# A hybrid decoder layer: half-width weight splits, a convolution tap on another engine, and moved value steps

## The reference, cut to what matters

```python
h  = rms_norm(x) * (1 + scale) + shift
z  = h @ w_in          # att q,k,v,gate | mLSTM q,k | v | o | gate | i,f | merge gates
# branch A: block-sparse softmax attention, 8 heads x 64
# branch B: 4 mLSTM heads, qk dim 128, v dim 256
qk = silu(causal_conv4(qk_pre, w_conv) + b_conv);  k = k * 128 ** -0.5
s  = (q @ k.T) * w;    num = s @ v;    den = s.sum(-1)
h  = num / maximum(abs(den), exp(-m));  h = rms_norm(h) * g * sigmoid(o)
C  = sum_s ws[s] * v[s] k[s]^T
u  = sigmoid(ga) * (ya @ w_att) + sigmoid(gm) * (ym @ w_mlstm);  y = x + gate * (u @ w_out)
```

## Time and profile before

| | us |
|---|---|
| runs shown | 815.5, 823.34, 824.85 |
| median | 823.34 |
| profiled execution | 820.3 |
| its span | 818.6 |
| TensorE busy in it | 728.3 |
| VectorE busy in it | 556.7 |

### The profile page before, as it was taken

How to read it: one execution, slowest core, us unless ns; L and a number is a source line. 1 busy time by engine, 2 the same in 40 slices (tenths; PEclk the granted TensorE clock), 3 DMA queues, 4 the chain that set the end, 5 groups by cost and what they waited for, 6 DMA issues and landing times.

```text
span 818.6 us, 14649 instructions
## 1 busy us (share of the span) xinstructions
PE 728.3 (89%) x5040; PEld 625.2 (76%) x5040; DVE 556.7 (68%) x501; ACT 311.6 (38%) x586; POOL 471.1 (58%) x204
## 2 busy tenths in 40 slices
PE   5889999798987969877999899997899999899993
PEld 1225888577765868776999889887789998899992
DVE  0150359989998897599699699879857458522342
ACT  1422463554526224324244343443232223323454
POOL 3035239446563852765966868678265646667552
PEclk9999799899896989989999999999799999999997
DMA  8974625688876891067557657569327535732202
GB/s 320 331 258 143 193 78 148 193 254 255 269 217 205 259 309 54 1 182 223 165 168 236 172 172 230 157 204 266 90 54 205 167 112 158 240 113 87 78 0 104
DMA packets 156902, 144.69 MB, mean 177 GB/s; under 512 B 7547, under 2 KB 115152, under 8 KB 156852
## 3 DMA queue, kind: packets, MB, share of 16 engines
q1 hardware_dynamic: 142696, 136.10, 55.5%
q10 hardware_dynamic: 14164, 8.07, 3.4%
HBM read 135.10 MB, written 9.11 MB: 176 GB/s over the span
## 4 chain that ended last, share of the span: by engine, by line
PE 34%; DVE 30%; issue 14%; SPq 7%; POOL 6%; DMA 4%; ACT 2%; DVEq 1%; POOLq 0%; ACTq 0%
PE ps L522 21%; DVE sb_arenaA L1600 5%; DVE sb_arenaA L1751 5%; DVE sb_arenaA L1756 4%; PE ps L540 4%; SPq L385 3%; DVE sb_arenaB L1756 3%; POOL sb_wL L1314 3%; SPq L386 3%; DMA sb_arenaA<-in_w_ada 2%; DVE sb_arenaB L1809 2%; DVE sb_arenaA L1604 2%; DVE sb_arenaB L1675 2%; SPq L369 1%; POOL sb_uL L1478 1%
## 5 line engine op out<-in xcount | busy, mean ns | idle before, releaser
L1314 POOL TENSOR_TENSOR sb_wL<-sb_wraw,sb_wH 128x1024 fp32r<-128x1024 f32 (+1 forms) x88 | 223.3, 2539 | 231.1 <-ACT sb_wH L929 222.6
L522 PE MATMUL ps<-sb_hH,sb_wH 128*128 128x260 f32 x1152 | 241.9, 292 | 4.3 <-POOL sb_wL L1314 2.5
L522 PE MATMUL ps<-sb_hL,sb_wH 128*128 128x260 f32 x1152 | 234.9, 286 | 0.0
L522 PE MATMUL ps<-sb_hH,sb_wL 128*128 128x260 f32 x1152 | 234.6, 286 | 0.0
L522 PEld LDWEIGHTS ps<-sb_hH,sb_wH 128*128 128x128 f32 x1152 | 182.0, 193 | 15.7 <-issue 11.9
L522 PEld LDWEIGHTS ps<-sb_hL,sb_wH 128*128 128x128 f32 x1152 | 181.3, 192 | 0.0
L522 PEld LDWEIGHTS ps<-sb_hH,sb_wL 128*128 128x128 f32 x1152 | 180.5, 192 | 0.0
L929 ACT ACTIVATE sb_wH<-sb_wraw 128x1024 fp32r<-128x1024 f32 (+1 forms) x88 | 90.3, 1026 | 228.9 <-PE ps L522 189.7
L1383 POOL TENSOR_TENSOR sb_arenaA<-sb_arenaA 128x2048 f32<-128x2048 f32 x32 | 117.7, 3682 | 10.1 <-DMA sb_arenaA<-in_cache_v 8.2
L1354 POOL TENSOR_TENSOR sb_arenaA<-sb_arenaA 128x2048 f32<-128x2048 f32 x12 | 61.5, 5122 | 35.8 <-DMA sb_arenaA<-in_cache_k 35.8
L1604 DVE TENSOR_REDUCE sb_arenaA<-sb_arenaA 128x2048 f32 (+1 forms) x32 | 72.5, 2280 | 6.8 <-POOL sb_arenaA L1354 4.6
(11 more groups left out here) (343 smaller groups left out, 1058.3 us busy)
## 6 DMA issues: line engine op xcount, KB each, us to landing
sb_wraw<-in_w_in SPq DMA_DIRECT2D x64, 512.0 KB, 4.8
sb_arenaA<-in_cache_k SPq DMA_DIRECT2D x128, 256.0 KB, 3.1
sb_arenaA<-in_cache_v SPq DMA_DIRECT2D x128, 256.0 KB, 3.2
sb_arenaA<-in_w_ada SPq DMA_DIRECT2D x6, 2048.0 KB, 8.8
sb_arenaB<-in_state_C SPq DMA_DIRECT2D x8, 512.0 KB, 3.8
sb_wraw<-in_w_mlstm SPq DMA_DIRECT2D x8, 512.0 KB, 4.1
sb_wraw<-in_w_out SPq DMA_DIRECT2D x8, 512.0 KB, 3.7
sb_arenaB<-in_x_prompt SPq DMA_DIRECT2D x1, 2048.0 KB, 18.2
```

The lines of the kernel that those rows point to most:

```text
L522: last = mm(ps[:, 2 * s + a, 0:HALF], w[:, s, k, :], x[:, k, a * HALF:(a + 1) * HALF], start=(k == 0 and w is wH and x is xH), stop=(k == ...
L1314: tt(wL[:, j % 2, 0:ks], wraw[:, j % 4, 0:ks], wH[:, j % 2, 0:ks].bitcast(F32), ALU.subtract)\
```

## The change

1. The copy of the keys (ScalarE, L1063) and the store of k stand ahead of the scaling of the values.
2. TensorE does tile 4 of the first mLSTM head ahead of the score sums (L828), and tile 5 ahead of L833.
3. `high` and `low` work in two halves of a tile each. The first half of a high part waits only for the first half of the tile two before (`z_half`), and TensorE waits for the second low half in the middle of its tile.
4. The first tap of each convolution, with the bias, is done by ScalarE (`first_tap`), and VectorE waits for it.
5. KSCALE is folded into L1782 and L1790; the two scalings of the keys and their semaphore are gone.
6. On VectorE the value pairs move within a head. In the loop: 6 (of the head before), weights and scores, copy, 0, weighted keys, 2, denominators, scaled output, 4, gate products, gated output. In the first head: 0, 2 and 4 all behind the scaled output.
7. On POOL each value step of the loop moves ahead of one low part: step 6, low 2, step 7, low 3, step 0, low 0, mask, step 1, low 1, step 2, low 2, step 3, low 3, step 4, low 0, step 5, low 1. In the first head step 4 moves ahead of the low part of tile T_ML+9 (tile 1 of the second head), and at the end step 6 ahead of a low part.

SP's order isn't changed. The core of the diff:

```diff
@@ -510,10 +511,13 @@
             tr = nc.tensor.transpose
 
             def ztile(j, n, xH, xL, ks=KT, part_ready=None):
-                pe.wait_ge(lo_done, n + 5)
+                pe.wait_ge(lo_done, 2 * n + 9)
                 pe.wait_ge(z_free, n + 1)
                 s = j % 2
                 for k in range(ks):
+                    if k == ks // 2:
+                        last.then_inc(z_half, 1)
+                        pe.wait_ge(lo_done, 2 * n + 10)
                     if part_ready:
                         pe.wait_ge(part_ready, 2 + k + 1)
                     for w, xs_ in ((wH, (xH, xL)), (wL, (xH,))):
...
@@ -732,7 +737,6 @@
                     ztile(3, n + 3, hH, hL)
                     pe.wait_ge(hn_ev, 4 * h + 1)
                 pe.wait_ge(sg_rdy, 2 * h + 2)
-                pe.wait_ge(qk_rdy, h + 1)
                 pe.wait_ge(ym_done, h + 1)
...
@@ -821,17 +825,17 @@
                     last = tr(ps[0:B, 5 + a, t * P:(t + 1) * P], qkvS[:, 1 + a, t, :], ident[:, :])
             last.then_inc(sel_pe, 1)
             ztile(3, T_ML + 3, hH, hL)
+            ztile(4, T_ML + 4, hH, hL)
 
             pe.wait_ge(ya_done, 1 + PAIRS)
             pe.wait_ge(sel_dve, 2)
             for b in range(B):
                 last = mm(ps[0:B, 7, 0:P], colsel[:, b, :], score[:, b * P:(b + 1) * P], start=(b == 0), stop=(b == B - 1))
             last.then_inc(sel_pe, 1)
-            ztile(4, T_ML + 4, hH, hL)
+            ztile(5, T_ML + 5, hH, hL)
 
             pe.wait_ge(sel_dve, 3)
             mm(ps[:, 7, :], ones[0:B, :], pend.rearrange("p b n -> p (b n)"), start=True, stop=True).then_inc(sel_pe, 1)
-            ztile(5, T_ML + 5, hH, hL)
             pe.wait_ge(sel_act, 1)
             mlstm(0, True)
             with pe.Fori(0, MH - 1) as h:
...
@@ -922,11 +926,13 @@
             chain = Chain(act, act_chain)
             f = nc.scalar.activation
 
-            def high(j, n, quad, ks=KT):
+            def high(j, n, quad, ks=KT, after_short=False):
 
                 act.wait_ge(ld_w[j % 4], 16 * (quad + 1))
-                act.wait_ge(z_done, n + 1)
-                f(wH[:, j % 2, 0:ks], wraw[:, j % 4, 0:ks], ACT.Copy).then_inc(hi_done, 1)
+                for half, used in ((0, z_done if after_short else z_half), (1, z_done)):
+                    part = slice(half * ks // 2, (half + 1) * ks // 2)
+                    act.wait_ge(used, n + 1)
+                    f(wH[:, j % 2, part], wraw[:, j % 4, part], ACT.Copy).then_inc(hi_done, 1)
 
             def leave(j, n, *dests):
                 act.wait_ge(z_done, n + 3)
...
@@ -1057,12 +1063,12 @@
                 high(3, n + 3, quad)
                 weights(0, t)
                 leave(0, n + 2, (vT, ACT.Copy))
-                normalise(0, t)
                 act.wait_ge(kn_mm, t + 1)
                 act.wait_ge(st_k, 16 * t + 16)
                 f(kN, ps[:, 7, :].rearrange("p (j n) -> p j n", j=TT), ACT.Copy).then_inc(kn_ev, 1)
                 act.wait_ge(kn_ev, t + 1)
                 act.dma_start(rows_out(O["k_p"], t), kN).then_inc(st_k, 16)
+                normalise(0, t)
                 high(0, n + 4, quad + 1)
                 if not before:
                     gate_exps()
...
@@ -1076,6 +1082,15 @@
                 leave(1, n + 3, (yaT[:, bass.ds(t, 1), :].rearrange("p o n -> p (o n)"), ACT.Silu))
                 high(1, n + 5, quad + 1)
                 weights(1, t)
+
+            def tap(j, e, h):
+                return vcol[:, bass.ds(h + (V_WC + KT * j + MH * e), 1)]
+
+            def first_tap(e, h):
+
+                act.wait_ge(z_free, T_ML + 8 * h + 3 + e)
+                f(cacc[:, e, :], pre[:, e, 0:T], ACT.Identity, scale=tap(0, e, h),
+                  bias=vcol[:, bass.ds(h + (V_BC + MH * e), 1)]).then_inc(tap_rdy, 1)
 
             attention(0, False)
             with act.Fori(0, PAIRS - 1) as t:
...
@@ -1102,6 +1117,9 @@
             act.wait_ge(ya_done, 1 + PAIRS)
             act.wait_ge(st_k, 16 * (1 + PAIRS))
             act.wait_ge(st_v, 16 * (1 + PAIRS))
+            act.wait_ge(v_one, 2)
+            for e in range(2):
+                first_tap(e, 0)
             for e in range(2):
                 act.wait_ge(cv_rdy, e + 1)
                 f(qkc[:, e, :], cacc[:, e, :], ACT.Silu).then_inc(sg_rdy, 1)
...
@@ -1138,7 +1156,9 @@
                     high(2, n + 2, quad)
                     leave(0, n, (pre[:, 0, 3:3 + NT], ACT.Copy))
                     high(3, n + 3, quad)
+                    first_tap(0, h)
                     leave(1, n + 1, (pre[:, 1, 3:3 + NT], ACT.Copy))
+                    first_tap(1, h)
                     decays(h, False)
                     for e in range(2):
                         act.wait_ge(cv_rdy, 2 * h + e + 1)
...
@@ -1310,11 +1330,13 @@
 
             def low(j, n, ks=KT):
 
-                pool.wait_ge(hi_done, n + 1)
-                tt(wL[:, j % 2, 0:ks], wraw[:, j % 4, 0:ks], wH[:, j % 2, 0:ks].bitcast(F32), ALU.subtract)\
-                    .then_inc(lo_done, 1)
-
-            pool.sem_inc(lo_done, 4)
+                for half in range(2):
+                    part = slice(half * ks // 2, (half + 1) * ks // 2)
+                    pool.wait_ge(hi_done, 2 * n + half + 1)
+                    tt(wL[:, j % 2, part], wraw[:, j % 4, part], wH[:, j % 2, part].bitcast(F32), ALU.subtract)\
+                        .then_inc(lo_done, 1)
+
+            pool.sem_inc(lo_done, 8)
             for slot in range(KV_SLOTS):
                 pool.sem_inc(page_free[slot], 1)
             pool.sem_inc(u_lo, 2)
...
@@ -1401,32 +1423,32 @@
             pool.wait_ge(sel_dve, 8)
             for s in range(4):
                 value_step(s, 0)
+            value_step(4, 0)
             low(1, T_ML + 9)
-            value_step(4, 0)
             value_step(5, 0)
             with pool.Fori(0, MH - 1) as i:
                 h = i + 1
                 n = T_ML + 8 * h
+                value_step(6, h - 1)
                 low(2, n + 2)
-                value_step(6, h - 1)
+                value_step(7, h - 1)
                 low(3, n + 3)
-                value_step(7, h - 1)
+                value_step(0, h)
                 pool.wait_ge(w_exp, h + 1)
                 low(0, n + 4)
                 causal_weights(h)
-                value_step(0, h)
+                value_step(1, h)
                 low(1, n + 5)
-                value_step(1, h)
+                value_step(2, h)
                 low(2, n + 6)
-                value_step(2, h)
+                value_step(3, h)
                 low(3, n + 7)
-                value_step(3, h)
+                value_step(4, h)
                 low(0, n + 8)
-                value_step(4, h)
+                value_step(5, h)
                 low(1, n + 9)
-                value_step(5, h)
+            value_step(6, MH - 1)
             low(2, T_GATE + 2)
-            value_step(6, MH - 1)
             value_step(7, MH - 1)
             for j in range(1, 4):
                 low((j + 2) % 4, T_GATE + j + 2)
...
@@ -1669,8 +1691,7 @@
                 def tap(j):
                     return vcol[:, bass.ds(h + (V_WC + KT * j + MH * e), 1)]
 
-                chain(v.tensor_scalar(acc, pre[:, e, 0:T], tap(0), vcol[:, bass.ds(h + (V_BC + MH * e), 1)],
-                                      ALU.mult, ALU.add))
+                dve.wait_ge(tap_rdy, 2 * h + e + 1)
                 for j in range(1, 4):
                     last = v.scalar_tensor_tensor(acc, pre[:, e, j:j + T], tap(j), acc, ALU.mult, ALU.add)
                     if j < 3:
...
@@ -1772,24 +1791,26 @@
                 if first:
                     choice_sums()
                 else:
-                    dve.wait_ge(sg_rdy, 2 * h + 2)
-                    v.tensor_scalar(qkc[:, 1, :], qkc[:, 1, :], KSCALE, None, ALU.mult).then_inc(qk_rdy, 1)
-
                     value_pair(6, h - 1, False)
                 dve.wait_ge(st_mm, h + 1)
                 dve.wait_ge(w_rdy, h + 1)
                 for k, b, c in ((0, 4, 0), (1, 5, 0), (3, 5, 384), (2, 6, 0)):
-                    last = tt(wt[:, k, 0:T - k * P], wt[:, k, 0:T - k * P], ps[:, b, c:c + T - k * P], ALU.mult)
+                    last = v.scalar_tensor_tensor(wt[:, k, 0:T - k * P], wt[:, k, 0:T - k * P], KSCALE,
+                                                  ps[:, b, c:c + T - k * P], ALU.mult, ALU.mult)
                 last.then_inc(mpt_rdy, 1)
                 dve.wait_ge(z_free, n + 6)
                 v.tensor_copy(vS[:, bass.ds(2 * h, 2), :], mvT[:, :, T:NT])
                 if first:
                     choice_normalise()
+                if not first:
+                    value_pair(0, h, first)
                 dve.wait_ge(kt_mm, h + 1)
                 dve.wait_ge(wsc_rdy, h + 1)
-                tt(kw, ps[:, 6, :].rearrange("p (j n) -> p j n", j=TT), over(wsc[:, :], P), ALU.mult)\
+                v.scalar_tensor_tensor(kw, ps[:, 6, :].rearrange("p (j n) -> p j n", j=TT), KSCALE, over(wsc[:, :], P),
```

(11 more changed lines are left out.)

17 lines of the change are left out of this document (9 added, 8 removed).

## The result

The changed kernel takes 827.15 us (median of 7, 825.93 to 829.96), the kernel before 822.24 (median of 7, 815.5 to 825.32). The change is slower by about 1%, where 839 (815 to 848) was forecast. The profiled execution has a span of 825.4 us, against 818.6 before.

What follows compares the result with a forecast made beforehand. TensorE was busiest (728.3 of 818.6 us), but VectorE set the mLSTM head's 65.6 us period. Terms: 820.3 + 11 (first head) + 6.8 (two heads) + 2.5 (gate stage) − 2 (attention) = 838.6, forecast 839, range 815 to 848.

Steps and rivals of the forecast that it cites:

- attention: Attention stage: key copy ahead of the scaling takes most of L696's 14.1 us wait, little returns; −2 us, bounds −5 and +3.
- tile ahead of the score sums: Ahead of the first mLSTM head: a tile of matmuls fills L828's 6.4 us wait; 4 us gained, bounds 0 and 6.4.
- first head, scores to scores: First mLSTM head: late page release and step 4 make head 1's scores later, +11 us net, bounds +4.7 to +12.2.
- two loop heads: Steady mLSTM heads: VectorE idles twice for POOL's steps and products are blocked; +3.4 us each, bounds −3.1 and +5.
- here the POOL edit bites: First mLSTM head: low half of tile T_ML+9 now stands behind late step 4; TensorE stands 12.5 us before tile 1.
- Into the gate stage: After the last mLSTM head: L1813 comes later, and L846's wait and the sample chain follow; +2.5 us, bounds 0 and +3.
- the case: Whole kernel: the prediction's main outcome, slower, chance 0.60, alone said to reach from 826 to 847 us.
- The signs: mLSTM heads: TensorE idles about 12 us, step 4 about 6 later, two VectorE idles per head, L738 distances 68 to 70.
- Rival A: mLSTM heads: POOL delivers steps in time, waits go, TensorE sets the period at 62.5; 810 us, chance 0.12.
- Rival B: mLSTM heads: even; first head pays only 4.7 us, each steady head is 1 shorter; 821 us, chance 0.22.
- Rival C: All stages: TensorE waits mid-tile for a low half, 0.6 us in every second of 64 tiles; 839 us, chance 0.06.

Runs made afterwards that it cites:

- repeated old orders: Second run of the changed kernel with VectorE's value sums and POOL's value steps in the order of before, in all heads; 801.67 us.

## Why the prediction was right or wrong

By its own terms, profile against profile:

| term | predicted | measured | from |
|---|---|---|---|
| attention | −2 | −9.9 | L816 284.69, now L820 274.83 |
| tile ahead of the score sums | −4 | −3.3 | to L742 of head 0: 30.5, now 27.2 |
| first head, scores to scores | +15 | +13.7 | 71.6, now 85.3 |
| two loop heads | +6.8 | +4.5 | 65.6, now 67.85 each |
| from L742 of head 3 to the end | +2.5 | +1.7 | 300.7, now 302.4 |
| sum | +18.3 | +6.7 | span +6.8 |

*The first head* (+11 with the tile's 4 in it, so +15) was right in mechanism and size. The denominators caught in POOL's row of steps, step 4 at 32.7 us behind the first step (measured 32.0), TensorE's wait of 12.5 (11.4): all stand in the rows above. The emphasis on "here the POOL edit bites" was wrong: with the low part put back ahead of step 4 the scores came only 1.7 us earlier. The step that decides is the release of the pages by pair 0, that is, the denominators ahead of it on VectorE.

*The loop heads* were right nearly row by row: the two idle times (6 and 6.3 forecast, 5.78 and 6.01 measured) with their causes, pages for step 3 and ScalarE's root ahead of the high part. Only the gate products were taken too long, with two full blocks and a half: one full block came (3.80, L1833) and two partial ones, and the head took 67.85 and not 69. The rule of the Trainium skill in "SBUF — State Buffer", "Who interferes with whom", held in the rows shown here, most sharply on the smallest products (3.54 us for 128x4 values). L1816 has only one input and was held up as well (1.79 us for 0.17), which the rule as the prediction put it doesn't cover.

*Into the gate stage* +2.5 was a guess, and its mechanism didn't show: the wait that was to grow shrank (L846's 5.50 us, now L850's 3.9). The next one, L855's of 2.9 us, now L859's, grew to 6.5, and the granted clock from 570 to 705 us was 0.92 and not 0.95. Split at the first L895 (now L899; 123.2 and 120.5 us from the end), the stretch is 4.4 us longer ahead of it and 2.7 shorter behind it, where 0 was forecast. How much of this is the clock stays open.

*Attention* is the term that was mis-sized, by 7.9 of the 11.6 us between the two sums. Its premise, "in that stage VectorE is the busier engine", isn't so. The stage before and after, and TensorE's wait for the scaled weights of the softmax, before and after:

```profile
76.00:285.00 209.00, 188.27 (x1213) 155.56 (x1211) 171.49 (x169) 95.08 (x197) 110.33 (x29) 0.91 0.70 209
```

```profile
76.00:275.00 199.00, 185.69 (x1225) 155.54 (x1223) 158.64 (x169) 96.73 (x215) 104.29 (x47) 0.93 0.74 219
```

```profile
PE ps L626 <- ACT sb_arenaB L1025: 2.1, 3, 0.9
```

```profile
PE ps L631 <- ACT sb_arenaB L1031: 9.9, 4, 3.5
```

TensorE is busy 188.27 of 209 us, VectorE 171.49. Of the 10 us, 7.4 are idle time of TensorE (20.7, now 13.3) and 2.6 are busy time, for about as many matmul records at a granted clock of 0.93 and not 0.91. The waits say what the key copy does: 11.7 us go from L696, and 7.8 come back at L631, since the scaling (L1031) now stands behind the copy. The 3.9 us left over are inside the forecast's −5 and +3. The rest, clock and halves, wasn't in the term. The halves were costed at nothing, on POOL's own time (two of 1.28 against 2.40), and what they do to VectorE's products beside POOL was left out, although the same rule had just been used against the change. How the rest divides between halves, clock and the spread of 8.5 us between profiles of one attention code stays open.

*The range.* By its own bounds the case reaches from 818 to 848.5 us, not from 826 to 847. The direction was earned in the heads, but that the kernel came out slower hangs on about 5 us: an attention that ends at 269.7, as in two profiles of the same code, would have taken them (an estimate from 274.83).

*The signs.* The wait ahead of tile 1 (11.44) and the two idle times per head came as listed. Step 4 came at 354.34 and not 6 us behind 357.79, since everything ahead of it was 13 us early, and the distances (68.0 and 67.7) lie at the lower edge of 68 to 70.

*Rival A* (the waits go, TensorE limits) is what the kernel does without the moved sums and steps: 798 to 802 us, faster than its 810. The Trainium skill's remark in "Perfetto Trace Analysis", "Optimizing Scalar/DVE Operations", on breaking up instructions points the same way as the halves' 5.7 us; that they work by ending bubbles is not shown. *Rival B* had each steady head 1 us shorter, and they were 2.3 longer. *Rival C* didn't occur: TensorE waited for a low part three times in all, 15.1 us with the 11.4 in them, where C needed a wait in every second tile.

## What to carry to other kernels

A sum that frees a transfer's buffer can be on the path even when its result isn't needed for long: before moving it behind small dependent products, count from its end to the next transfer's landing and to what is queued behind that. Where one engine's instruction holds up another's, as POOL's did VectorE's here, cost it not only by its own time but by how long it can hold up the other; splitting POOL's and ScalarE's weight copies was worth 5.7 us, while the tap taken off VectorE earned nothing that could be told. Moving a copy ahead of another moves a wait as well: look for who waits for the one that is now behind. Compare an experiment's profile with all profiles of the same code before believing a difference of a few us. And test a bundle of edits apart: here five of them gained 2.4 and 1.3% in two groups of runs, and the reordering lost more than that.

## What the runs showed of the hardware

Executions with like waits and the same work took different times in a stretch, and the granted clock differed with them. The last head with the key copy alone, and in the kernel before (columns as above, the clock is the third from the end):

```profile
513.00:572.00 59.00, 51.19 (x377) 47.62 (x376) 48.61 (x27) 22.70 (x39) 46.55 (x17) 0.91 0.64 189
```

```profile
518.00:574.00 56.00, 48.81 (x376) 45.95 (x376) 48.74 (x26) 22.87 (x39) 46.43 (x17) 0.99 0.70 201
```

At 0.91 the stretch took 59 us and TensorE's 377 matmul records 51.19, at 0.99 it took 56 and 376 records 48.81. That is 3 of the 7 us by which the key copy's profile had been ahead. The same stretch without halves and in the repeated old orders:

```profile
503.00:563.00 60.00, 52.08 (x380) 48.21 (x378) 45.98 (x27) 23.73 (x40) 46.52 (x17) 0.92 0.69 200
```

```profile
501.60:556.70 55.10, 48.38 (x378) 45.86 (x377) 44.59 (x26) 23.59 (x46) 48.13 (x24) 0.99 0.73 213
```

Here the clock of 0.92 against 0.99 goes with 4.9 us. TensorE had the same 5 us wait behind this head in all four. What decides when the clock falls wasn't tried, so differences of 3 to 5 us between two single profiles mean little in such a stretch; the medians above carry the verdicts.
